# Attention of a hybrid decoder: turned weights and value products one tile behind the scores, value products with V stationary, the next head's projection in two-step pieces

## The reference

```python
def _diff_attn(...):            # two score maps of depth 32 per head
    s = einsum('bhcqd,bhckd->bhcqk', qi, k) * scale
    p = softmax(where(mask, s, NEG), axis=-1)
    w = p[:, :, 0] - lam * p[:, :, 1]
    o = einsum('bhqk,bhkv->bhqv', w, v)
    return _rmsnorm(o, gain) * (1.0 - lam_init)

def _fox_attn(...):             # one score map of depth 64 per head
    s = einsum('bhqd,bhkd->bhqk', qi, k) * scale + di[..., :, None] - D[:, :, None, :]
    p = softmax(where(mask, s, NEG), axis=-1)
    o = einsum('bhqk,bhkv->bhqv', p, v)
    return _rmsnorm(o, gain)
```

## Time and profile before

| | |
|---|---|
| median of 3 runs (lowest to highest) | 4002.17 us (3993.94 to 4009.2) |
| the profiled execution's own time | 4012.46 us |
| its span in the trace | 4010.6 us |
| PE busy, PEld busy | 3402.5 us (85%), 2224.4 us (55%) |
| DVE, ACT, POOL busy | 1671.6, 772.4, 122.1 us |
| mean granted clock of TensorE | 0.865 |
| attention, layer 0 and layer 1 | from 548.7 and from 2555.6 us, some 557 us each |

### The profile page before, as it was taken

One profiled execution on the slowest core, in us unless ns is written; L12 is line 12 of the kernel. 1 busy time (PEld: TensorE's weight loads), 2 busy tenths in 40 slices (PEclk: granted clock), 3 DMA queues, 4 the chain that ended last, 5 costly groups with the idle time before them and its releaser, 6 DMA issues.

```text
span 4010.6 us, 45134 instructions
## 1 busy us (share of the span) xinstructions
PE 3402.5 (85%) x14852; PEld 2224.4 (55%) x14852; DVE 1671.6 (42%) x2375; ACT 772.4 (19%) x1758; POOL 122.1 (3%) x131
## 2 busy tenths in 40 slices
PE   6999788788897499999769997887889974999994
PEld 3666456666743255555436664566667432555552
DVE  4777523333323223322267775233343232232234
ACT  2222223332211011111022222232322110111111
POOL 2100000000000100000100000000000001000002
PEclk9999996667798799999979999966676987999997
DMA  9400100000100899999820001000001008999996
GB/s 266 133 21 10 38 11 6 6 1 11 43 3 0 330 407 406 410 410 412 313 98 21 21 10 38 11 6 6 1 11 43 3 0 327 407 403 411 412 410 258
DMA packets 141070, 615.41 MB, mean 153 GB/s; under 512 B 13720, under 2 KB 48024, under 8 KB 123032
## 3 DMA queue, kind: packets, MB, share of 16 engines
q1 hardware_dynamic: 104952, 495.89, 31.4%
q0 software_dynamic: 16944, 60.89, 4.7%
q10 hardware_dynamic: 19056, 57.16, 3.8%
HBM read 538.34 MB, written 75.56 MB: 153 GB/s over the span
## 4 chain that ended last, share of the span: by engine, by line
PE 76%; DVE 7%; issue 6%; DMA 5%; ACT 3%; POOL 1%; ACTq 1%; DVEq 0%; SPq 0%; POOLq 0%
PE ps L1087 7%; PE ps L1000 7%; PE ps L978 7%; PE ps L1136 6%; PE ps L1233 6%; PE ps L1333 6%; PE ps L1323 6%; PE ps L1292 5%; PE ps L1298 4%; DMA arena<-xg 3%; PE ps L1151 3%; PE ps L1350 3%; PE ps L1199 3%; PE ps L1044 3%; PE ps L1069 3%
## 5 line engine op out<-in xcount | busy, mean ns | idle before, releaser
L1087 PE MATMUL ps<-arena 128*128 128x64 f32 (+2 forms) x1440 | 326.7, 378 | 47.0 <-ACT arena L723 27.7
L1087 PEld LDWEIGHTS ps<-arena 128*128 128x128 f32 (+2 forms) x1440 | 285.7, 278 | 111.0 <-issue 55.8
L1000 PE MATMUL ps<-arena 128*128 128x352 f32 (+1 forms) x768 | 275.5, 519 | 20.8 <-DVE rounded L1523 19.6
L978 PE MATMUL ps<-arena 128*128 128x512 f32 (+1 forms) x768 | 260.8, 498 | 5.4 <-DVEq L500 3.2
L1534 DVE TENSOR_REDUCE negmax<-ps 16x1 f32<-16x16 f32 (+8 forms) x216 | 151.0, 702 | 265.4 <-PE ps L1049 264.6
L1292 PE MATMUL ps<-arena 128*128 128x512 f32 x560 | 254.0, 607 | 2.6 <-ACT arena L900 2.6
L1136 PE MATMUL ps<-arena 128*128 128x256 f32 (+1 forms) x1152 | 251.6, 380 | 0.0
L1233 PE MATMUL ps<-arena 128*128 128x512 f32 (+1 forms) x576 | 251.1, 594 | 0.0
L1333 PE MATMUL ps<-arena 128*64 128x256 f32 x2240 | 249.5, 381 | 0.0
L1298 PE MATMUL ps<-arena 128*128 128x256 f32 x1120 | 247.4, 379 | 0.0
L1323 PE MATMUL ps<-arena 128*128 128x512 f32 x560 | 246.1, 592 | 0.0
(11 more groups left out here) (299 smaller groups left out, 4248.6 us busy)
## 6 DMA issues: line engine op xcount, KB each, us to landing
arena<-w SPq DMA_DIRECT2D x210, 2048.0 KB, 12.9
xg<-arena POOLq DMA_DIRECT2D x51, 512.0 KB, 12.3
arena<-xg ACTq DMA_DIRECT2D x39, 512.0 KB, 10.2
xg<-arena ACTq DMA_DIRECT2D x35, 512.0 KB, 7.5
arena<-w_in SPq DMA_DIRECT2D x16, 1024.0 KB, 5.7
arena<-xg ACTq DMA_DIRECT2D x35, 256.0 KB, 11.1
xg<-arena ACTq DMA_DIRECT2D x70, 128.0 KB, 9.3
arena<-w_in SPq DMA_DIRECT2D x16, 512.0 KB, 4.2
```

What stands on the lines that cost most here:

```text
L978: mm = pe.matmul(dst[0:hi - lo, a:b], w[:, k, lo:hi], uT[:, k, a:b], start=(k == 0), stop=(k == KD - 1))
L1000: mm = pe.matmul(out, w_qk[b][:, k, :], uT[:, k, lo:hi], start=(k == 0), stop=(k == KD - 1))
L1087: mm = pe.matmul(ps[0:r, 7, at:at + AW], WT[0:rows(i), g % 3, m * P:m * P + r], V[0:rows(i), i, n * AW:(n + 1) * AW], start=(i == 0), stop ...
```

## The change

- `turn_weights`, its copy `turned` and `outputs` of a tile move one iteration back: iteration t turns tile t - 1 and multiplies its bundles but the last, and makes the last bundle of tile t - 2. `attend_pe` and `attend_act` run two iterations more, `attend_dve` one. The buffers of the exponentials grow from three to four.
- `outputs` (now L1118): V is stationary (128 x 64), the turned weights move (128 columns). The result stands with its 64 values on partitions; `copy_out` (ACT, L742) copies it unscaled to `OT`. Once a head, in the next head's tile 1, PE turns `OT` back with one transpose (piece `o`) and four (piece `g`, L1020), and DVE scales them by the reciprocals into `ah`. The squares follow in tile 1, the scaling in tile 2 (before: 0 and 1).
- Five points in an iteration (0 to 4). `a` is cut into four pieces of two contraction steps (L1034), so that scores, turns and outputs stand between them. `PLAN_DA` and `PLAN_FX` take the place of the old tables.
- Waits for `bank2`, and those of `outputs`, are separate instructions (`wait_alone`).
- The selection matrices move into the place of `gamma`; its load for the second norm moves from before HGRN2 to the middle of the FX heads, ahead of the load of the output projection's weights.

```diff
-DURING_DA = {(0, 0): "a0", (0, 2): "b0", (1, 0): "a1", (1, 1): "c0", (1, 2): "d0", (2, 0): "e0", (2, 1): "f0",
-             (2, 2): "b1", (3, 0): "a2", (3, 1): "c1", (3, 2): "d1", (4, 0): "e1", (4, 1): "f1", (4, 2): "b2",
-             (5, 0): "c2", (5, 2): "d2", (6, 0): "e2", (6, 2): "f2"}
-DURING_FX = {(0, 0): "a0", (1, 0): "a1", (2, 0): "a2"}
+PLAN_DA = {0: ["a0.0", "a0.1", "a0.2", "a0.3", "b0"], 2: ["a1.0", "a1.1", "a1.2", "a1.3", "c0"],
+           3: ["d0", "e0", "f0", "b1", None], 4: ["a2.0", "a2.1", "a2.2", "a2.3", "c1"],
+           5: ["d1", "e1", "f1", "b2", None], 6: ["c2", "d2", "e2", "f2", None]}
+PLAN_FX = {0: ["a0.0", "a0.1", "a0.2", "a0.3", None], 2: ["a1.0", "a1.1", "a1.2", "a1.3", None],
+           4: ["a2.0", "a2.1", "a2.2", "a2.3", None]}
...
 def piece_at(n, j, slot):
+    if 1 <= n < ALL and j == 1:
+        return {3: "o", 4: "g"}.get(slot)
...
                 def copy_out(t):
-                    act.activation(ah[n % 2][0:r, j, :], ps[0:r, 7, at:at + AW], ACT.Copy,
-                                   scale=rinv[0:r, 2 * j:2 * j + 1]).then_inc(t_oc, 1)
+                    act.activation(turned_out(j), ps[0:AW, 7, at:at + rows(j)], ACT.Copy).then_inc(t_oc, 1)
...
                 for t in range(TILES + 2):
                     if new:
                         exps(new[0])
                     piece_act(layer, n + 1, piece_at(n, j, 0))
+                    if t >= 2:
+                        copy_out(t - 2)
+                    piece_act(layer, n + 1, piece_at(n, j, 1))
+                    if mine:
+                        turned(t - 1, 0)
                     for u in new[1:]:
                         exps(u)
...
                     for m, i in enumerate(bundles(j)[b]):
-                        mm = pe.matmul(ps[0:r, 7, at:at + AW], WT[0:rows(i), g % 3, m * P:m * P + r],
-                                       V[0:rows(i), i, n * AW:(n + 1) * AW], start=(i == 0), stop=(i == j),
+                        mm = pe.matmul(ps[0:AW, 7, at:at + r], V[0:rows(i), i, n * AW:(n + 1) * AW],
+                                       WT[0:rows(i), g % 3, m * P:m * P + r], start=(i == 0), stop=(i == j),
                                        skip_group_check=True)
...
-                for t in range(TILES):
+                for t in range(TILES + 2):
+                    if new:
+                        scores(new[0])
                     piece_pe(layer, n + 1, piece_at(n, j, 0))
-                    if t:
-                        outputs(t - 1, len(bundles((t - 1) % T)) - 1)
-                    turn_weights(t, 0)
+                    if t >= 2:
+                        outputs(t - 2, len(bundles((t - 2) % T)) - 1)
                     piece_pe(layer, n + 1, piece_at(n, j, 1))
-                    for b in range(1, len(bundles(j))):
-                        turn_weights(t, b)
-                        outputs(t, b - 1)
+                    if 1 <= t <= TILES:
+                        turn_weights(t - 1, 0)
+                    piece_pe(layer, n + 1, piece_at(n, j, 2))
+                    if not late:
+                        for u in new[1:]:
+                            scores(u)
+                    piece_pe(layer, n + 1, piece_at(n, j, 3))
+                    if 1 <= t <= TILES:
+                        for b in range(1, len(bundles((t - 1) % T))):
+                            turn_weights(t - 1, b)
+                            outputs(t - 1, b - 1)
```

More of the change, by code:

```diff
@@ L204, in build @@
         causal = sb("causal", [P, P])
-        gamma = sb("gamma", [P, D])
+        with nc.sbuf_tensor("gamma", [P, D], F32) as gamma:
+            pass
+        gamma_r = sb("gamma_r", [P, D], F32R)
         gain_hg = sb("gain_hg", [P, DEPTH, HW])
@@ L310, in build @@
         s = Place(SCRATCH + at)
-        powers = [s.take(L) for _ in range(3)]
+        powers = [s.take(L) for _ in range(4)]
         ffx = powers[0][0:HEADS]
-        raw, rot = s.take(wide), s.take(wide)
+        raw = s.take(wide)
         V = s.take(T, 2 * HEADS * AW)
@@ L539, in _ @@
                 if stop > 1:
-                    load_gamma(A["norm_ffn"][layer])
                     def load_qk(n):
@@ L748, in attend_act @@
+                    piece_act(layer, n + 1, piece_at(n, j, 4))
+                    if HEADS - 1 <= n < ALL - 1 and j == (6 if n < HEADS else 5):
                         decay_act(layer, n + 1)
-                copy_out(TILES - 1)
                 head_rstd(t_ss, t_a, t_rstd, layer * ALL + ALL - 1, AW)
@@ L987, in piece_pe @@
                     return
-                kind, x = piece[0], int(piece[1])
+                kind = piece[0]
+                for semaphore, value in bank2:
+                    wait_alone(pe, semaphore, value)
+                bank2.clear()
+                if kind in "og":
+                    done = (layer * ALL + n - 2) * 2
+                    if kind == "o":
+                        wait_alone(pe, t_oc, ONE + layer * TILES + (n - 1) * T)
+                        pe.transpose(ps[0:META, 2, 0:AW], OT[0:AW, 4 * P:4 * P + META], ident[0:AW, 0:AW])\
+                          .then_inc(t_row, 1)
+                    else:
+                        for p in range(4):
+                            mm = pe.transpose(ps[:, 2, p * P:(p + 1) * P], OT[:, p * P:(p + 1) * P], ident[:, :])
+                        mm.then_inc(t_row, 1)
+                    bank2.append((t_ah, ONE + done + (1 if kind == "o" else 2)))
+                    return
+                x = int(piece[1])
                 (lo, hi), ops = CUTS[x], operands_of(n)
                 out = ps[:, 2, 0:hi - lo]
-                for semaphore, value in bank2:
-                    pe.wait_ge(semaphore, value)
-                bank2.clear()
+                part = [2 * int(piece[3]), 2 * int(piece[3]) + 1] if "." in piece else range(KD)
                 if kind == "a":
@@ L996, in piece_pe @@
                     nth = n // 2 + 1 if n < HEADS + 2 else n - 2
-                    if x == 0:
+                    if x == 0 and 0 in part:
                         pe.wait_ge(t_w[b], layer * (48 if b == 0 else 80) + nth * 16)
-                    for k in range(KD):
-                        mm = pe.matmul(out, w_qk[b][:, k, :], uT[:, k, lo:hi], start=(k == 0), stop=(k == KD - 1))
+                    for k in part:
+                        mm = pe.matmul(out, w_qk[b][:, k, :], uT[:, k, lo:hi], start=(k == 0), stop=(k == KD - 1),
+                                       skip_group_check=True)
+                    if KD - 1 not in part:
+                        return
                     mm.then_inc(t_proj, 1)
@@ L1584, in attend_dve @@
                 peak(1)
[L1585 removed]
+                for t in range(TILES + 1):
                     n, j = divmod(t, T)
[L1587 removed]
+                    new = ahead(t) if t < TILES else []
+                    mine = t >= 1 and (t - 1) // T >= HEADS
                     if new:
                         peak(new[0])
+                    piece_dve(layer, n + 1, piece_at(n, j, 0))
                     if n < HEADS:
                         join(t)
[L1592 removed]
+                    elif t < TILES:
                         v.wait_ge(t_P, ONE + U0 + LAST[t] + 1)
[L1594 to L1595 removed]
+                        st.made(v.reciprocal(rinv_a[0:rows(j), n % 2, 2 * j:2 * j + 1], rowsum[0:rows(j), 2 * j:2 * j + 1]))
+                    piece_dve(layer, n + 1, piece_at(n, j, 1))
+                    if mine:
+                        turned(t - 1, 0)
                     for u in new[1:]:
                         peak(u)
[L1598 to L1604 removed]
+                    piece_dve(layer, n + 1, piece_at(n, j, 2))
+                    piece_dve(layer, n + 1, piece_at(n, j, 3))
+                    if mine:
+                        for b in range(1, len(bundles((t - 1) % T))):
+                            turned(t - 1, b)
+                    piece_dve(layer, n + 1, piece_at(n, j, 4))
+                    if 1 <= n < ALL and j == 1:
                         finish_squares(n - 1)
[L1606 removed]
+                    if 1 <= n < ALL and j == 2:
                         finish(n - 1)
@@ L1803, in copy_mT @@
                          .then_inc(p_tv, 1)
+                    v.wait_ge(s_gamma, layer * 32 + 32)
                     copy_mT(0)
```

136 lines of the change are left out of this document (72 added, 64 removed).

## The result

The kernel before took 4007.86 us (median of 12 runs, 3993.94 to 4013.34), the changed one 3967.21 us (12 runs, 3945.04 to 3987.96). The ratio is 0.9895, with a 95% interval of 0.9877 to 0.9913: 41 us faster, where the forecast was 181 us faster. The profiled execution took 3980.23 us, with a span of 3978.0 us.

The account below looks back on a forecast made before the run. PE was taken to bound the kernel, through its lowered clock in attention and its idle time. Heads costed as work / clock + idle summed to 463.6 us a layer against 554.6; 176 us less in both layers gave 3826 us, range 3720 to 3960.

Parts of the forecast that it names:

- 2.6 us idle: DA heads, tiles 7 and 8: PE waits for the turned copy behind the next exponential, 4.1 us with 1.5 of work.
- another 3.4: DA heads, tile 8: the last bundle's copy stands behind the second exponential, 3.4 us more idle time.
- 3.3 us, less 0.6 of work: DA heads, tile 6: `d2` waits for ACT's eviction of `c2` behind the exponential of tile 7's first unit.
- 3.3 again: DA heads, tile 6: `f2` waits 3.3 us for the eviction of `e2` behind the second exponential.
- took nothing for the outputs: All heads: the new output pair costs the same as the old; bounds 3 us gain to 3 us loss a head.
- FX heads have a copy on DVE behind one peak: FX heads: few waits remain, so idle time of 8.7, 9.3 and 7.4 us becomes 5 to 6.
- the 6 that the prediction named as a sign of being wrong: FX heads: PE waiting more than 6 us for copies would show the prediction wrong.
- 324.6 forecast: One layer's eight heads: busy time times clock, with 47.0 us for heads 1 and 2, 39.0 to 41.8 for 4 to 6.
- so 0.95: FX heads: the clock rises from about 0.74 to 0.95, as the form held 1.00 in HGRN2.
- so 0.84: DA heads: the clock rises from 0.65 to only 0.84, with long waits in tiles 1 and 6 to 8.
- Rival B: Attention: the clock rises in FX heads only, DA heads keep 0.65; 25 us gain a layer, 3952 us, chance 0.17.
- C: DA heads, tiles 6 to 8: bank 2's chain behind exponentials, clock doesn't rise; slower, 4028 us, chance 0.08.

Follow-up runs that it names:

- e1_oldform: The changed kernel with outputs in the old form (turned weights stationary, V moving 64 columns, no turning back): 3976.25 us, ratio 0.9914.
- e4_actorder: The changed kernel with ACT's evictions, copy-out and some turned copies ahead of the next tile's exponentials, and one DVE peak moved later: 3784.6 us, ratio 0.944.
- e9_evict: The changed kernel with only ACT's evictions at points 0 and 2 ahead of the exponentials, and DVE's second peak later: 3915.32 us, ratio 0.9755.
- e8_evictcopy: The changed kernel with ACT's evictions at points 0 and 2 and the copy-out ahead of the exponentials, and DVE's second peak later: 3833.85 us, ratio 0.9582.
- e11_filler: The changed kernel with two unread float32 products of 128 columns added on PE ahead of each tile's turns: 3975.56 us, ratio 0.9918.

## Why the prediction was wrong

**The direction and the places of the waits: right.** `join` vanished from PE's waits. "2.6 us idle" and "another 3.4" in tiles 7 and 8 became 1.00 and 3.02; in tile 6 `d2` was forecast at "3.3 us, less 0.6 of work" and waited 1.57, `f2` at "3.3 again" and waited 2.77; piece `o` was forecast at 4 and took 3.1. Idle time of the eight heads is 102.5 us in layer 0 and 103.5 in layer 1, where the forecast's terms sum to 96.

**The output pair costs the same, the form doesn't.** The forecast took nothing for the outputs. For the pair that is right: eight pairs of one bundle took 1.23 us at the upper and 2.13 at the lower level, against 1.24 and 2.15. What it left out is the step from a bundle to the next operation. Before, then now, at the upper level:

```profile
1088.78 1.24 PE L1087 MATMUL ps<-arena 16*128 16x64 f32 x8
1089.86 0.71 PE L1069 MATMUL ps<-ident,arena 128*16 128x128 f32 x5
...
726.22 1.23 PE L1118 MATMUL ps<-arena 16*64 16x128 f32 x8
727.38 0.33 PE L1106 MATMUL ps<-ident,arena 128*128 128x128 f32 x1
```

From the start of the bundle to the next operation it is 1.08 us before and 1.16 now; at the lower level 1.91 (706.66 to 708.57) and 2.05 (715.57 to 717.62). With 15 bundles a head, 120 a layer, 0.08 us each make 10 us, an estimate from these rows.

**Idle time of the FX heads: a missed wait.** "FX heads have a copy on DVE behind one peak" left out ACT. The first output bundle of a tile also waits for the copy-out of the tile before it, which the change puts behind the next unit's exponential: 4.9 us in head 5, 8.9 idle against 5 forecast. The order of ACT's program was in the diff; I costed the turned copies by it and not the copy-out. With DVE's L1613 (2.2 us) the outputs of head 5 wait 7.1 us for copies, over the 6 that the prediction named as a sign of being wrong.

**Work: somewhat small.** Busy time times clock sums to 336 us in layer 0, head by head, against 324.6 forecast. At the forecast's mean clock of 0.883 (324.6 us of work in 463.6 - 96 of busy time) that is 13 us. It is the form's: with it alone taken back, e1_oldform has 18 to 22 us less of this product a layer. The bundles account for 10 of them by the estimate above; the turning back was forecast at 0.6 us a head, and the rest is open.

**The clock: the step that failed.** "An FX head after the change is ... of the form that held 1.00 in HGRN2, with idle time only in tile 1, so 0.95. A DA head has long waits in tiles 1 and 6 to 8, so 0.84." Measured 0.76 to 0.87 and 0.72 to 0.74 in layer 0, 0.79 to 0.92 and 0.74 to 0.82 in layer 1. With 336 us of work, a mean clock of 0.761 instead of 0.883 makes 441 us busy instead of 381: 60 of the 80 us that layer 0 misses, with 13 for the work and 6.5 for the idle time. Layer 1 misses 61.6 us. I took form and waits as if each acted on the clock in its own measure. The table shows that they act together: the new form is worth 9 us beside the waits and 72 without them. HGRN2's stretch was no fair model, since inside it no wait was longer than 0.3 us; and the waits of the DA heads I had listed, without pricing them twice. Rival B, 3952 us, came nearest in time, by luck and not by its mechanism: in it the DA heads keep the old clock and the FX heads reach 0.95. The DA heads rose a little instead (0.65 to 0.73), and the FX heads rose far less than it said.

That e4_actorder has the forecast's mechanism without most of those waits is shown by its numbers: work 56.9 x 0.90 = 51.2 us in head 2, idle 11.8, a clock of 0.90 where 0.84 was forecast, and FX heads 4 to 6 at 0.97 to 1.00 for 0.95 (0.88 to 1.00 in layer 1).

The rule of the Trainium skill that spoke for C (TensorE: Matmul & The Clock Gate, section "A second HAM failure mode: psum-queue depth-cycling") did better than I credited it. In the changed kernel the clock stood at 0.57 from piece `d2` in tile 6 of head 2 on into head 3, with PE waiting 1.57 and 2.77 us for bank 2 and 1.00 and 3.02 us for turned copies (the first of these ends where the stretch begins):

```profile
777.59:801.00 23.41, 16.61 (x67) 12.97 (x68) 7.99 (x13) 6.77 (x17) 0.00 (x0) 0.57 0.00 1
```

But e4_actorder hands the same bank over as often, and in the same stretch, from `d2` on into head 3, where its longest wait is 1.21 us, the clock held:

```profile
730.52:746.38 15.86, 12.47 (x81) 9.33 (x82) 9.22 (x18) 9.10 (x22) 0.00 (x0) 1.00 0.00 1
```

So the rule agrees with the changed kernel and not with e4_actorder: the handover itself doesn't bring the clock down. What differs here is the length of the waits, and with it the share of time that PE is busy (16.61 of 23.41 us against 12.47 of 15.86). That share doesn't decide by itself, since the earlier trace rows have 0.50 with 12.89 of 15.70 us busy. A long wait alone doesn't bring it down either: ahead of HGRN2's stretch in the kernel before, PE waited 2.9 us and the clock stood at 1.00 throughout:

```profile
409.40:412.40 3.00, 0.08 (x2) 0.02 (x2) 2.21 (x4) 2.30 (x3) 0.00 (x0) 1.00 0.39 103
```

## What to carry to other kernels

When work is moved behind or ahead by a tile on the bounding engine, the order of every engine that empties its PSUM has to move with it: an eviction or copy that PE needs in the same iteration goes ahead of an operation whose input is yet to be made, even where that engine is busy a fifth of the time or a third. A part that brings nothing alone can be worth 130 us once another wait is out of its way, so parts are judged against the order in which they will run, not by undoing them one at a time. A wait on TensorE can cost twice, as idle time and as the clock of the work around it; here the second was the larger, 81 of 109.8 us.

## What the runs showed that I had not expected

- The clock can turn on very little. In head 5, e9_evict and e8_evictcopy have the same instructions on every engine and differ in one place of ACT's order; 1.6 us less idle time (8.9 to 7.3) went with 12.8 us less busy time, and the clock rose from 0.76 to 0.97. It did so in both layers.
- Work without use can pay for itself. In e11_filler head 6 had 36 more weight loads on PE (282 for 246) and took 7.3 us less in layer 0 and 8.2 in layer 1. What exactly the clock answers to, length of the waits or columns streamed in between, these runs don't separate.
- The same FX head can run at different clocks from layer to layer of one execution (head 5: 66.3 us at 0.76 in layer 0, 56.6 us at 0.92 in layer 1), with the same program. So the clock of one head is a sample, and a reading of one head counts only where the other layer repeats it; sums over a layer are steadier, though they too differ by 18.5 us in this execution (543.7 and 525.2).
